# Two blocks of a transformer: retention's input projections moved into the steps of stick-breaking attention

## The chip, the cores and the metric

One core of a Trainium2 chip runs the whole program. The metric is the device time of one execution in microseconds; the median of the runs is compared. The five engines are called TensorE (PE in the profile; PEld is its weight load), VectorE (DVE), ScalarE (ACT), GpSimd (POOL) and SyncE (SP, which here only issues DMAs).

## The reference, cut to what matters

Two transformer blocks over 512 tokens of width 1024 in fp32. The part around the change is the mixing layer of the second block: one projection to 3584 columns, which are seven groups of 512, then two kinds of attention with eight heads of 64 each.

```python
xn = _rmsnorm(x, g_mix_norm)
proj = xn @ w_in                       # sb_q sb_k sb_v r_q r_k r_v r_g, 512 columns each
q_a, k_a = _rmsnorm(heads(sb_q)), _rmsnorm(heads(sb_k))
# stick-breaking, per head and block of 128 queries:
z = q_a @ k_a.T / 8;  mask = key < query
lneg = where(mask, log_sigmoid(-z), 0)
w = where(mask, exp(log_sigmoid(z) + reverse_cumsum(lneg) - lneg), 0);  y_a = w @ sb_v
q_b = _rope(_rmsnorm(heads(r_q)));  k_b = _rope(_rmsnorm(heads(r_k))) / 8
y_b = _group_norm(_retention(q_b, k_b, heads(r_v))) * silu(r_g)
x = x + concatenate([y_a, y_b]) @ w_out
```

After it come a top-4 mixture of 32 experts and a gated embedding. Before it comes the first block (two attentions and an MLP).

## The kernel before, in words

The program is one core's five instruction streams, written out by hand, with semaphores between them. Each engine works its stream in order. The 512 tokens are four tiles of 128 (NT). Matrix products of the projections are made in three parts: the operands are split into a top and a remainder (`half_top`, `ring_low`; `hT_top`, `hT_low`) and `three` (L1473) issues top times top, top times remainder and remainder times top.

**The projection.** The weights of one group of 512 columns are a chunk ("win2", c), 2 MB, loaded by SP into slots 0 and 1 of a ring in turn (`place`). A slot is loaded again when the chunk in it has been multiplied. Each chunk has two halves of four row blocks. ScalarE makes a half's top (`top`, L1033, four ACTIVATEs at L1043), VectorE its remainder in place (`low`, L2117, four instructions at L2126), and TensorE multiplies (`project`, L1479): four products of three parts for each of the four token tiles, 48 products a half, 96 a chunk. The tops lie in pairs of places listed in `TOP_AT`. Each of the four results has a PSUM bank, from which ScalarE copies it to SBUF with the row's norm factor (`copy_out`, L989, its ACTIVATE at L995).

The order of the chunks (`IN2`) is stick-breaking's q and k, retention's q and k, stick-breaking's v, retention's v and g. The loop over the seven chunks stands at L1785 (TensorE) and L1264 (ScalarE). After the fourth chunk TensorE turns stick-breaking's q and k into columns (`pairs_T`, "sbT"), which ScalarE copies to sbqT and, in halves of 64 partitions, to sbkz (L1282). After the seventh it turns retention's q and k ("rT"), copied to rqT and rkT. VectorE meanwhile normalises the heads (`heads`, L2150: square, sum, reciprocal of the root that ScalarE takes in `roots`, product), multiplies retention's by their gains (L2561), turns them (`rope`, L2160, six instructions of 128x256 a tile) and takes the mean off retention's v (L2577 to L2579).

**Stick-breaking attention** is `attention(2, ...)` on three engines. It runs over steps s = 0 to 40. In step s, TensorE makes the scores of step s (L1607; query tile t = s // 8, head s % 8, (t+1) x 128 keys), turns the weights of step s-3 (t+1 transposes, L1524) and multiplies those of step s-5 with v (L1625). VectorE adds the mask to the scores (L2208) and, in `stick` (L2173), scans (L2181) and multiplies (L2182) for step s-1. ScalarE takes two sigmoids of step s (L1082, L1083) and copies the turned weights of step s-4 (L1090). At each eighth step VectorE copies a tile's outputs (L2221), TensorE turns them ("oT"), ScalarE makes their top (L1106) and VectorE their remainder (L2141).

**What sets the order.** The list `order` gives each PSUM result a bank by hand or in rotation; `acquire` makes TensorE wait until the result before it in this bank has been taken. In this attention the scores have banks 0, 1, 2, 6 in turn, the transposes 3 and 4, the outputs 5 and the turned outputs 7. The buffers of the scan (sbl, sbw) are four each. While steps 1 to 8 run, VectorE also multiplies retention's k and turned q by their decay (`while_sticking`, L2586). ScalarE's Silu of the gate (L1288) stands ahead of the attention.

**Around it.** SP loads the embedding's tokens and weights (ptok, ple) when the last chunk has been multiplied, and the norm rows (gnrow) and the first output chunk when the last score has been made. GpSimd sets parts of sbkz to zero after the fourth chunk and of the retention's states after the sixth. After the attention TensorE turns the tokens, then does the retention's scores (`ret_scores`, L1806).

## Time and profile before

| what | value |
|---|---|
| runs | 2386.22, 2377.54, 2377.66 us |
| median | 2377.66 us |
| span of the profiled execution | 2375.5 us, from its first to its last instruction |
| its own time | not listed apart; the two lower runs are 2.0 and 2.2 us above this span |
| TensorE busy | 2239.7 us, 94% |
| VectorE busy | 1808.9 us, 76% |
| ScalarE busy | 1393.7 us, 59% |
| GpSimd busy | 209.7 us, 9% |
| mean granted TensorE clock | 0.967 |

The profile comes from one execution. A record of a matmul begins when it starts and ends by a model, so neighbouring records overlap and a pace is read from starts. The granted clock is a share of full speed, 1.00 being 2.4 GHz and 0.50 being 1.2 GHz. The seven chunks are projected from about 756 to 913 us, stick-breaking attention runs from 917 to 986 us, the retention after it to about 1030 us, and the experts take the time from about 1120 to 2330 us.

### The profile page before, as it was taken

Reading aid. Unit: us, or ns where it says so; the run is one execution under the profiler, and the core shown is the slowest. Engines: PE = TensorE matmul, PEld = TensorE weight load, DVE = VectorE, ACT = ScalarE, POOL = GpSimd, SP = SyncE. Lnnn points to the kernel's source line nnn. Section 1 sums busy time; section 2 is a strip of 40 time slices with the busy share of each in tenths; the row PEclk is TensorE's granted clock in tenths of the full one; section 3 lists DMA queues with packets and bytes.
Section 4 is the critical chain, followed back from the end, with each engine's and each line's share of the span. In section 5 each row is a group of like instructions: output and inputs, shape, how many; then the busy total and the mean of one; then the engine's idle time right before and its main releaser. Section 6 shows DMA issues by size and latency. Waiting matters only on the chain.

```text
span 2375.5 us, 30478 instructions
## 1 busy us (share of the span) xinstructions
PE 2239.7 (94%) x10453; PEld 1808.7 (76%) x10453; DVE 1808.9 (76%) x1917; ACT 1393.7 (59%) x1564; POOL 209.7 (9%) x175
## 2 busy tenths in 40 slices
PE   5998897999999998976999999999999999999998
PEld 3866676888788886755788888888888888888866
DVE  7887635555634585766899999999999999999964
ACT  4355525333413344433778778778778778778753
POOL 1000000000000000000241111011111111111100
PEclk8999798999999998987999999999999999999999
DMA  9530312333022310154999999999999999999960
GB/s 336 178 128 1 124 36 74 103 107 102 32 98 71 122 71 27 54 173 165 370 394 392 385 390 377 392 386 385 386 386 386 388 382 387 386 384 382 387 240 36
DMA packets 185074, 570.40 MB, mean 240 GB/s; under 512 B 10508, under 2 KB 34991, under 8 KB 184975
## 3 DMA queue, kind: packets, MB, share of 16 engines
q1 hardware_dynamic: 172239, 523.69, 57.6%
q0 software_dynamic: 12768, 45.81, 7.0%
q8 instruction: 43, 0.70, 0.1%
q14 instruction: 24, 0.20, 0.0%
HBM read 543.24 MB, written 26.23 MB: 240 GB/s over the span
## 4 chain that ended last, share of the span: by engine, by line
PE 51%; DVE 1%; issue 1%; ACT 0%; DMA 0%; ACTq 0%; DVEq 0%; POOLq 0%
PE bank L1936 11%; PE bank L1938 11%; PE bank L1942 11%; PE bank L1931 4%; PE bank L1929 4%; PE bank L1930 4%; PE bank L1524 3%; PE bank L1957 1%; PE bank L1543 0%; PE bank L1544 0%; PE bank L1545 0%; PE bank L2018 0%; PE bank L2012 0%; DMA rows<-hn_rows,idx_in 0%; PE bank L1980 0%
## 5 line engine op out<-in xcount | busy, mean ns | idle before, releaser
L2712 DVE TENSOR_TENSOR w_lo<-stage,w_hi 128x2048 fp32r<-128x2048 f32 x396 | 885.7, 2285 | 55.2 <-ACT w_hi L1342 55.2
L1342 ACT ACTIVATE w_hi<-stage 128x2048 fp32r<-128x2048 f32 x396 | 740.5, 1920 | 80.8 <-PE bank L1942 52.5
L1936 PE MATMUL bank<-w_hi,xeT_hi 128*128 128x512 f32 x792 | 261.7, 412 | 0.0
L1938 PE MATMUL bank<-w_hi,xeT_lo 128*128 128x512 f32 x792 | 245.8, 391 | 0.0
L1942 PE MATMUL bank<-w_lo,xeT_hi 128*128 128x512 f32 x792 | 212.2, 390 | 0.0
L1545 PE MATMUL bank<-half_top,hT_low 128*128 128x512 f32 (+1 forms) x480 | 187.9, 391 | 0.0
L1938 PEld LDWEIGHTS bank<-w_hi,xeT_lo 128*128 128x128 f32 x792 | 149.4, 189 | 32.5
L1936 PEld LDWEIGHTS bank<-w_hi,xeT_hi 128*128 128x128 f32 x792 | 147.6, 190 | 33.7 <-issue 0.3
L1942 PEld LDWEIGHTS bank<-w_lo,xeT_hi 128*128 128x128 f32 x792 | 149.1, 188 | 31.1
L1543 PE MATMUL bank<-half_top,hT_top 128*128 128x512 f32 (+1 forms) x416 | 162.7, 391 | 5.0 <-DVE ring_low L2128 2.2
L1544 PE MATMUL bank<-ring_low,hT_top 128*128 128x512 f32 (+1 forms) x416 | 161.8, 389 | 0.0
L1745 PE MATMUL bank<-hT_hi,up_hi 128*128 128x512 f32 x352 | 137.8, 392 | 7.0 <-issue 7.0
L1747 PE MATMUL bank<-hT_hi,up_lo 128*128 128x512 f32 x352 | 137.7, 391 | 0.0
L1746 PE MATMUL bank<-hT_lo,up_hi 128*128 128x512 f32 x352 | 137.6, 391 | 0.0
L2128 DVE TENSOR_TENSOR ring_low<-ring,half_top 128x2048 fp32r<-128x2048 f32 (+2 forms) x28 | 61.0, 2186 | 99.7 <-ACT half_top L1045 99.5
L1045 ACT ACTIVATE half_top<-ring 128x2048 fp32r<-128x2048 f32 (+2 forms) x28 | 51.0, 1829 | 139.2 <-PE bank L1545 134.7
L1936 PE MATMUL bank<-w_hi,eaT_hi 128*128 128x512 f32 x396 | 125.0, 397 | 0.9 <-DVE eaT_lo L2784 0.9
L1938 PE MATMUL bank<-w_hi,eaT_lo 128*128 128x512 f32 x396 | 122.0, 389 | 0.0
L1545 PEld LDWEIGHTS bank<-half_top,hT_low 128*128 128x128 f32 x480 | 91.9, 191 | 18.3
L1942 PE MATMUL bank<-w_lo,eaT_hi 128*128 128x512 f32 x396 | 105.8, 389 | 0.0
L1352 ACT ACTIVATE el<-bank,one 128x512 f32<-128x512 f32 x66 | 45.5, 689 | 98.3 <-PE bank L1931 98.3
L1931 PE MATMUL bank<-w_lo,xeT_hi 128*128 128x512 f32 x264 | 102.8, 389 | 0.0
(495 smaller groups left out, 4213.2 us busy)
## 6 DMA issues: line engine op xcount, KB each, us to landing
stage<-in_w_up_gate SPq DMA_DIRECT2D x264, 1024.0 KB, 7.4
stage<-in_w_down SPq DMA_DIRECT2D x132, 1024.0 KB, 7.3
ring<-in_w_ada SPq DMA_DIRECT2D x12, 2048.0 KB, 9.4
ring<-in_w_up SPq DMA_DIRECT2D x22, 1024.0 KB, 7.7
ring<-in_w_in SPq DMA_DIRECT2D x10, 2048.0 KB, 7.9
ring<-in_w_out SPq DMA_DIRECT2D x4, 2048.0 KB, 11.0
ring<-in_w_down SPq DMA_DIRECT2D x4, 2048.0 KB, 8.6
stage<-in_w_ple_gate SPq DMA_DIRECT2D x4, 1024.0 KB, 7.8
```

Of the source, the lines that this page charges most:

```text
L1342: fn(w_hi[top_of(h)][:, :], src[:, :], ACT.Copy).then_inc(s_hi, 1)
L1543: mm(b, hi, wh, start=first, stop=False)
L1544: mm(b, hi, wl, start=False, stop=False)
L1545: return mm(b, lo, wh, start=False, stop=last)
L1745: mm(b[:, :], wh, hTs[0][:, k, :], start=k == 0, stop=False)
L1746: mm(b[:, :], wh, hTs[1][:, k, :], start=False, stop=False)
L1747: ins = mm(b[:, :], wl, hTs[0][:, k, :], start=False, stop=k == KT - 1)
L1931: ins = mm(bank[b][:, :], hi[:, k0 + k, :], wl[:, k, cs], start=False, stop=k == kn - 1)
L1936: mm(bank[b][:, :], hi[:, k0 + k, :], wh[:, k, at_[b]:at_[b] + CW], start=first and k == 0, stop=False)
L1938: mm(bank[b][:, :], lo[:, k0 + k, :], wh[:, k, at_[b]:at_[b] + CW], start=False, stop=False)
L1942: ins = mm(bank[b][:, :], hi[:, k0 + k, :], wl[:, k, at_[b]:at_[b] + CW], start=False, stop=False)
L2712: tt(w_lo[h][:, :], stage[h][:, :], w_hi[top_of(h)][:, :].bitcast(FP), ALU.subtract).then_inc(s_lo, 1)
```

## The change

The three chunks of stick-breaking attention (q, k, v) are projected first, as before. The four chunks of retention (q, k, v, g) are then projected inside the attention's steps 0 to 31: `BESIDE` gives each step one chunk, half and token tile, twelve products, which TensorE issues at the end of its step. ScalarE's copies, tops and two roots, and VectorE's remainders, norms, gains, rotations and mean, are spread over the steps too. So that banks 2, 4, 6 and 7 are free for the four results of a chunk, scores have banks 0 and 1, transposes bank 3, and turned outputs bank 1. The scan's buffers are two instead of four. ScalarE copies the turned weights ahead of its two sigmoids. The turned outputs of the first three tiles are stored (`stick_out`) and split at steps 34 and 35. Retention's q and k are turned in steps 36 and 37, the decays follow in VectorE's steps 38 and 39, and Silu stands in ScalarE's step 33. SP's waits read as before, though the last chunk that they name now ends with step 31.

```diff
@@ -209,13 +209,13 @@
+    sbl = [at(R + (8 + 2 * i) * KB, [P, S], name=f"sbl{i}") for i in range(2)]
+    sbw = [at(R + (12 + 2 * i) * KB, [P, S], name=f"sbw{i}") for i in range(2)]
+    stick_out = [at(R + (84 + 2 * i) * KB, [P, 4, P], name=f"stick_out{i}") for i in range(3)]
...
-    sbl = [at((32 + 2 * i) * KB, [P, S], name=f"sbl{i}") for i in range(4)]
-    sbw = [at((88 + 2 * i) * KB, [P, S], name=f"sbw{i}") for i in range(4)]
@@ -356,7 +356,7 @@
-    IN2 = [0, 1, 3, 4, 2, 5, 6]
+    IN2 = [0, 1, 2, 3, 4, 5, 6]
@@ -429,19 +429,30 @@
+    BESIDE = [(c, h, t) for c in range(3, 7) for h in range(2) for t in range(NT)]
+    TURNED = {36: 0, 37: 1}
+    RQ_AT = (9, 10, 12, 13, 14, 15, 16, 18)
+    RK_AT = (19, 20, 22, 23, 24, 25, 26, 29)
...
-                product(("S", kind, s), (0, 1, 2, 6)[s % 4] if kind == 2 else s % 3)
+                product(("S", kind, s), s % 2 if kind == 2 else s % 3)
...
-                product(("T", kind, i), 3 + i % 2)
+                product(("T", kind, i), 3 if kind == 2 else 3 + i % 2)
...
-                product(("oT", kind, (s - OT_LAG[kind]) // H - 1), 7)
+                product(("oT", kind, (s - OT_LAG[kind]) // H - 1), 1 if kind == 2 else 7)
+            if kind == 2 and s < len(BESIDE):
+                c, h, t = BESIDE[s]
+                if h == 0:
+                    product(("win2", c, t), (2, 4, 6, 7)[t])
+            if kind == 2 and s in TURNED:
+                for t in range(NT):
+                    product(("rT", TURNED[s], t), ((2, 4, 6, 7) if TURNED[s] == 0 else (0, 4, 6, 7))[t])
@@ -494,16 +505,12 @@
-    for c in range(7):
+    for c in range(3):
...
-        if c == 3:
-            for qk in range(2):
-                for t in range(NT):
-                    product(("sbT", qk, t))
...
-            product(("rT", qk, t))
+            product(("sbT", qk, t))
@@ -1088,6 +1085,17 @@
+                    if kind == 2 and s < 4 * H:
+                        n = (s // H + 1) * P
+                        W1 = sbl[s % 2]
+                        act_e.wait_ge(s_msk, s + 1)
+                        b = bank[bank_of[("S", 2, s)][0]]
+                        if s >= 2:
+                            act_e.wait_ge(s_P, 4 * H + s - 1)
+                        if s >= 4:
+                            full(act_e, ("T", 2, s - 4))
+                        fn(PR[s % 4][:, 0:n], b[:, 0:n], ACT.Sigmoid)
+                        take(fn(W1[:, 0:n], b[:, 0:n], ACT.Sigmoid, scale=-1.0), ("S", 2, s))
@@ -1101,6 +1109,8 @@
+                elif kind == 2 and t < 3:
+                    take(fn(stick_out[t][:, :, :], blk3(b[:, :]), ACT.Copy), label)
@@ -1261,32 +1271,55 @@
-            for c in range(7):
-                if c < 6:
-                    top(("win2", c + 1), 0)
+            def mix_rows(c, t):
+                copy_out(win2_dst(c, t), ("win2", c, t), scale=stat[:, 48 + t:49 + t])
+            for c in range(3):
+                top(("win2", c + 1), 0)
...
-                    copy_out(win2_dst(c, t), ("win2", c, t), scale=stat[:, 48 + t:49 + t])
-                if c < 6:
-                    top(("win2", c + 1), 1)
-                if c < 3:
+                    mix_rows(c, t)
+                top(("win2", c + 1), 1)
+                if c < 2:
...
-                if c == 3:
-                    act_e.wait_ge(s_qs, 1)
+            act_e.wait_ge(s_qs, 1)
+            for t in range(NT):
+                copy_out(sbqT[:, :, t * P:(t + 1) * P], ("sbT", 0, t), lambda b: blk3(b[:, :]), qs[:, 0:1])
+            for t in range(NT):
+                label = ("sbT", 1, t)
+                b = full(act_e, label)
+                for par in range(2):
+                    hp = slice(par * HD, (par + 1) * HD)
+                    ins = fn(sbkz[hp, par::2, t * P:(t + 1) * P], blk3(b[hp, :]), ACT.Copy, scale=vec[hp, VSK:VSK + 1])
+                take(ins, label)
+            def while_sticking(s):
+                if 1 <= s <= len(BESIDE):
+                    c, h, t = BESIDE[s - 1]
+                    if h:
+                        if (c, t) == (6, 0):
+                            act_e.wait_ge(s_nrm, 9)
+                        mix_rows(c, t)
+                if s % 8 == 0 and 8 <= s < 32:
+                    top(("win2", 3 + s // 8), 1)
+                if s % 8 == 4 and s < 24:
+                    top(("win2", 4 + s // 8), 0)
+                if s in (11, 20):
+                    roots(7 + s // 20)
+                if s == 33:
...
-                        copy_out(sbqT[:, :, t * P:(t + 1) * P], ("sbT", 0, t), lambda b: blk3(b[:, :]), qs[:, 0:1])
+                        taken(act_e, ("win2", 6, t))
+                    fn(rg[:, :, :], rg[:, :, :], ACT.Silu).then_inc(s_sg, 1)
+                if s == 34:
+                    full(act_e, ("win2", 6, NT - 1))
+                    for t in range(3):
+                        fn(out_top[0][:, :, t * P:(t + 1) * P], stick_out[t][:, :, :], ACT.Copy).then_inc(s_ohi, 1)
+                if s - 1 in TURNED:
+                    qk = TURNED[s - 1]
...
-                        label = ("sbT", 1, t)
-                        b = full(act_e, label)
-                        for par in range(2):
-                            hp = slice(par * HD, (par + 1) * HD)
-                            ins = fn(sbkz[hp, par::2, t * P:(t + 1) * P], blk3(b[hp, :]), ACT.Copy, scale=vec[hp, VSK:VSK + 1])
-                        take(ins, label)
-                    roots(8)
-            for qk in range(2):
-                for t in range(NT):
-                    copy_out(rT[qk][:, :, t * P:(t + 1) * P], ("rT", qk, t), lambda b: blk3(b[:, :]))
-            fn(rg[:, :, :], rg[:, :, :], ACT.Silu).then_inc(s_sg, 1)
-            attention(2, PR2, PT2)
+                        copy_out(rT[qk][:, :, t * P:(t + 1) * P], ("rT", qk, t), lambda b: blk3(b[:, :]))
+            attention(2, PR2, PT2, while_sticking)
@@ -1782,21 +1815,39 @@
-            for c in range(7):
+            for c in range(3):
...
-                if c == 3:
-                    for qk, src in enumerate((sbq, sbk)):
-                        pe.wait_ge(s_nrm, 6 + qk)
-                        pairs_T("sbT", qk, src)
-            for qk, src in enumerate((rq, rk)):
-                pe.wait_ge(s_nrm, 8 + qk)
-                pairs_T("rT", qk, src)
+            for qk, src in enumerate((sbq, sbk)):
+                pe.wait_ge(s_nrm, 6 + qk)
+                pairs_T("sbT", qk, src)
...
+            def while_sticking(s):
+                if s < len(BESIDE):
+                    c, h, t = BESIDE[s]
+                    label = ("win2", c, t)
+                    if t == 0:
+                        pe.wait_ge(s_low, half_no[("win2", c), h] + 1)
+                    _, wl, wh, kn, n = half_cols(("win2", c), h)
+                    b = bank[bank_of[label][0]] if h else acquire(label)
+                    for k in range(kn):
+                        kk = h * kn + k
+                        ins = three(b[:, 0:n], of(hT_top[2])(kk, t), of(hT_low)(kk, t), wh[:, k * n:(k + 1) * n], wl[:, k * n:(k + 1) * n], kk == 0, kk == KT - 1)
+                    if h:
+                        publish(ins, label)
+                    elif t == NT - 1:
+                        ins.then_inc(s_read, 1)
+                if s in TURNED:
+                    qk = TURNED[s]
+                    pe.wait_ge(s_nrm, 8 + qk)
+                    pairs_T("rT", qk, (rq, rk)[qk])
...
-                      lambda h, j: sbv[:, j, h * HD:(h + 1) * HD], PR2, PT2, o2)
+                      lambda h, j: sbv[:, j, h * HD:(h + 1) * HD], PR2, PT2, o2, while_sticking)
@@ -1864,6 +1915,7 @@
+            pe.wait_ge(s_olo, NT + 3)
@@ -2136,6 +2188,9 @@
+                if kind == 2 and t < 3:
+                    tt(hT_low[:, 0:4, cols_t], stick_out[t][:, :, :], out_top[0][:, :, cols_t].bitcast(FP), ALU.subtract).then_inc(s_olo, 1)
+                    return
@@ -2174,10 +2229,10 @@
-                W1, W2, A = sbl[s % 4], sbw[s % 4], PR2[s % 4]
+                W1, W2, A = sbl[s % 2], sbw[s % 2], PR2[s % 4]
...
-                if s >= 4:
-                    dve.wait_ge(s_P, 4 * H + s - 3)
+                if s >= 2:
+                    dve.wait_ge(s_P, 4 * H + s - 1)
@@ -2224,7 +2279,7 @@
-                    if kind and s >= H + OT_LAG[kind] and (s - OT_LAG[kind]) % H == 0:
+                    if kind and s >= H + OT_LAG[kind] and (s - OT_LAG[kind]) % H == 0 and (kind == 1 or s == 4 * H + OT_LAG[kind]):
@@ -2552,45 +2607,78 @@
-                low(("win2", 2 + j), 0, 1)
-            for j, (a, c) in enumerate(((rq, 2), (rk, 3))):
-                for t in range(NT):
-                    taken(dve, ("win2", c, t))
-                link(heads(7 + j, a, tmpr, scale=None if j == 0 else HD ** -0.5))
+                if j == 0:
+                    low(("win2", 2), 0, 1)
+                else:
+                    low(("win2", 3), 0)
+            rvh = rv[:, :, :].rearrange("p t (h d) -> p (t h) d", d=HD)
+            vmean = hs[:, 4 * 32:5 * 32]
+            rk3 = rk[:, :, :].rearrange("p t (h d) -> p t h d", h=H)
+            def ret_heads(j, n):
+                a, c = ((rq, 3), (rk, 4))[j]
+                st = hs[:, (7 + j) * 32:(8 + j) * 32]
...
-                link(tt(flat, flat, bc(grow2[:, j, :], 1, [P, 32, HD]), ALU.mult))
-                low(("win2", 4 + j), 0)
-                for t in range(NT):
+                squares = tmpr[:, :].rearrange("p (n d) -> p n d", d=HD)
+                if n == 0:
+                    for t in range(NT):
+                        taken(dve, ("win2", c, t))
+                    link(tt(squares, flat, flat, ALU.mult))
+                elif n == 1:
+                    link(ve.reduce_sum(st, squares, axis=AX))
+                    ts(st, st, 1.0 / HD, EPS, ALU.mult, ALU.add).then_inc(s_ms, 1)
+                elif n == 2:
+                    dve.wait_ge(s_rt, 8 + j)
+                    link(ve.reciprocal(st, st))
+                    if j:
+                        link(ts(st, st, HD ** -0.5, None, ALU.mult))
+                    link(tt(flat, flat, bc(st, 2, [P, 32, HD]), ALU.mult))
+                elif n == 3:
+                    link(tt(flat, flat, bc(grow2[:, j, :], 1, [P, 32, HD]), ALU.mult))
+                elif n < 4 + NT:
+                    t = n - 4
...
-                ins.then_inc(s_nrm, 1)
-                dve.wait_ge(s_nrm, 8 + j)
-                low(("win2", 4 + j), 1)
-            low(("win2", 6), 0, 1)
-            for t in range(NT):
-                taken(dve, ("win2", 5, t))
-            rvh = rv[:, :, :].rearrange("p t (h d) -> p (t h) d", d=HD)
-            vmean = hs[:, 4 * 32:5 * 32]
-            link(ve.reduce_sum(vmean, rvh, axis=AX))
-            link(ts(vmean, vmean, 1.0 / HD, None, ALU.mult))
-            link(tt(rvh, rvh, bc(vmean, 2, [P, 32, HD]), ALU.subtract))
-            for t in range(NT):
-                full(dve, ("rT", 1, t))
-            rk3 = rk[:, :, :].rearrange("p t (h d) -> p t h d", h=H)
-            for t in range(NT):
-                taken(dve, ("rT", 0, t))
+                    else:
+                        ins.then_inc(s_nrm, 1)
+                        dve.wait_ge(s_nrm, 8 + j)
...
-                if 1 <= s <= NT:
-                    t = s - 1
-                    tt(rk3[:, t], rk3[:, t], bc(cb("kdec"), 2, [P, H, HD]), ALU.mult).then_inc(s_kd, 1)
-                elif NT < s <= 2 * NT:
-                    cols_t = slice((s - NT - 1) * P, (s - NT) * P)
-                    tt(rqdT[:, :, cols_t], rT[0][:, :, cols_t], blk3(cb("qdec")), ALU.mult).then_inc(s_rqd, 1)
+                if s % 8 == 1 and s < 26:
+                    low(("win2", 3 + s // 8), 1)
+                if s % 8 == 5 and s < 24:
+                    low(("win2", 4 + s // 8), 0)
+                if s in RQ_AT:
+                    ret_heads(0, RQ_AT.index(s))
+                if s in RK_AT:
+                    ret_heads(1, RK_AT.index(s))
+                if s == 27:
+                    for t in range(NT):
+                        taken(dve, ("win2", 5, t))
+                    link(ve.reduce_sum(vmean, rvh, axis=AX))
+                    link(ts(vmean, vmean, 1.0 / HD, None, ALU.mult))
+                if s == 28:
+                    link(tt(rvh, rvh, bc(vmean, 2, [P, 32, HD]), ALU.subtract))
+                if s == 35:
+                    full(dve, ("win2", 6, NT - 1))
+                    for t in range(3):
+                        out_low(2, t)
+                if s == 38:
+                    for t in range(NT):
+                        taken(dve, ("rT", 0, t))
+                    for t in range(NT):
+                        cols_t = slice(t * P, (t + 1) * P)
+                        tt(rqdT[:, :, cols_t], rT[0][:, :, cols_t], blk3(cb("qdec")), ALU.mult).then_inc(s_rqd, 1)
+                if s == 39:
+                    for t in range(NT):
+                        full(dve, ("rT", 1, t))
+                    for t in range(NT):
+                        tt(rk3[:, t], rk3[:, t], bc(cb("kdec"), 2, [P, H, HD]), ALU.mult).then_inc(s_kd, 1)
```

## Rows read from the trace of the kernel before

**Rows 1.** Busy time of each engine while one chunk is projected; last: clock, DMA share, GB/s

```profile
821.30:843.00 21.70, 21.70 (x98) 17.94 (x97) 17.88 (x21) 7.98 (x13) 0.00 (x0) 1.00 0.28 97
```

**Rows 2.** The same view in stick-breaking attention

```profile
916.60:931.80 15.20, 6.21 (x31) 4.93 (x29) 9.05 (x26) 9.43 (x23) 0.00 (x0) 0.65 0.17 69
...
959.00:975.60 16.60, 15.55 (x92) 10.23 (x91) 15.50 (x24) 11.41 (x25) 0.00 (x0) 1.00 0.01 1
...
975.60:988.80 13.20, 11.54 (x84) 10.36 (x82) 6.79 (x10) 6.11 (x12) 0.00 (x0) 0.90 0.57 200
```

**Rows 3.** Waits from 912 to 990 us: total us, times, longest

```profile
PE bank L1524 <- DVE probs L2182: 7.3, 5, 6.0
...
PE bank L1524 <- ACT probsT L1090: 6.0, 10, 2.1
```

**Rows 4.** Timeline, TensorE: start, us, engine, line, instruction, count

```profile
907.79 0.39 PE L1543 MATMUL bank<-half_top,hT_top 128*128 128x512 f32 x1
...
908.47 0.39 PE L1543 MATMUL bank<-half_top,hT_top 128*128 128x512 f32 x1
...
914.98 1.91 PE L1524 MATMUL bank<-cona,rk 128*128 128x128 f32 x16
...
973.10 1.08 PE L1607 MATMUL bank<-sbkz,sbqT 128*128 128x512 f32 x2
...
982.37 2.85 PE L1625 MATMUL bank<-sbv,probsT 128*128 128x64 f32 x24
```

**Rows 5.** Timeline, VectorE in the attention's steps

```profile
924.31 0.29 DVE L2208 TENSOR_TENSOR bank<-bank,conb 128x128 f32<-128x128 f32 x1
...
925.16 0.68 DVE L2590 TENSOR_TENSOR rk<-rk,conb 128x512 f32<-128x512 f32 x1
...
967.41 1.22 DVE L2181 TENSOR_TENSOR_SCAN sbw<-sbl,one 128x512 f32<-128x512 f32 x1
...
969.50 1.22 DVE L2181 TENSOR_TENSOR_SCAN sbw<-sbl,one 128x512 f32<-128x512 f32 x1
```

**Rows 6.** Timeline, VectorE beside the projection

```profile
829.42 2.29 DVE L2146 TENSOR_REDUCE hs<-tmpr 128x32 f32<-128x2048 f32 x1
...
837.26 2.74 DVE L2126 SCALAR_TENSOR_TENSOR ring_low<-ring,vec,half_top 128x512 fp32r<-128x512 f32 x4
...
839.92 0.42 DVE L2166 TENSOR_TENSOR tmpr<-rq,trig 128x256 f32<-128x256 f32 x1
...
842.67 0.43 DVE L2166 TENSOR_TENSOR tmpr<-rq,trig 128x256 f32<-128x256 f32 x1
```

**Rows 7.** Timeline, ScalarE: copies, a half's top, and the turned keys

```profile
821.28 0.69 ACT L995 ACTIVATE rq<-bank,stat 128x512 f32<-128x512 f32 x1 [2.03 <-PE bank L1545]
...
843.63 2.55 ACT L1043 ACTIVATE half_top<-ring,vec 128x512 fp32r<-128x512 f32 x4
...
848.36 5.61 ACT L1282 ACTIVATE sbkz<-bank,vec 64x512 f32<-64x512 f32 x8
```

**Rows 8.** Timeline, ScalarE: Silu and the table load behind it

```profile
919.34 1.91 ACT L1288 ACTIVATE rg<-rg 128x2048 f32<-128x2048 f32 x1
...
921.27 1.28 ACT L1082 ACT_TABLE_LOAD   x1
```

**Rows 9.** Busy times by stretch, after TensorE's idle time at 1054 to 1062

```profile
1064.00:1068.00 4.00, 4.00 (x10) 3.09 (x10) 3.93 (x9) 1.43 (x1) 0.00 (x0) 0.50 0.00 0
```

**Rows 10.** Timeline, TensorE after two idle times (in brackets)

```profile
1062.34 0.80 PE L1543 MATMUL bank<-half_top,out_top 128*128 128x512 f32 x1 [8.22 <-DVE ring_low L2128]
...
1152.46 0.60 PE L1957 MATMUL bank<-bias,hot 96*128 96x512 bf16 x2 [3.61 <-DVE hot L2861]
...
1155.09 1.05 PE L1938 MATMUL bank<-w_hi,xeT_lo 128*128 128x512 f32 x2
```

**Rows 11.** DMA issues by line: count, KB each, us to landing

```profile
ring<-in_w_in SPq DMA_DIRECT2D x10, 2048.0 KB, 7.9
```

**Rows 12.** Timeline, TensorE: the first retention scores

```profile
988.81 2.02 PE L1806 MATMUL bank<-rqT,rkT 64*128 64x128 f32 x16
```

25 lines of the change are left out of this document (7 added, 18 removed).

## The prediction

> **What bounds the kernel now.** I read the busy shares by stretch first. While the second block's seven 512-column chunks are projected, TensorE never rests: a chunk of 96 products takes 21.7 us at full clock [rows 1]. From 916.7 to 988.8 us, in stick-breaking attention, it does rest: 9 of the first 15.2 us, 1 of the 16.6 us with the widest tiles, less than 2 of the last 13.2 [rows 2]. The waits name the cause: the transposes (L1524) wait for VectorE's product of probabilities (L2182) and for ScalarE's copy out of the transposes' bank (L1090) [rows 3]. So the two stages have opposite limits, and about 72.1 us of attention hold some 15 us of idle TensorE at most. I take 821.3 us (end of the third chunk's products) to 988.8 us (first retention score), 167.5 us, as the stretch that the change rebuilds; before it nothing moves on TensorE, and after it the same work follows.
>
> **TensorE's own work.** Products start every 0.227 us, three in 0.68, and each is 0.39 long, so a group's record ends up to 0.2 after its pace. With that off, 16 transposes in 1.91 are 0.11 each, the score of four blocks of 128 columns in 1.08 is 0.22 a block, and 24 PV products in 2.85 are 0.115 each, two to a block, 0.23 [rows 4]. A step of query tile t (0 to 3) has t+1 blocks of each, 0.56(t+1), and twelve products, 2.72 us plus about 0.03. With the transposes three steps behind and PV five behind, the eight steps of each tile take 25.0, 29.5, 34.5 and 39.0 us: **128.0 us** for 32 steps.
>
> **VectorE's work per step.** Mask, scan and product recur every 0.86 us for one block (924.31 to 925.16) and 2.09 for four [rows 5]; between them 1.27 and 1.66 by the width. To that the change adds, per step: a half's remainder (seven halves, one at each of steps 1, 5, 9, 13, 17, 21, 25) 2.66; a pass over 128x2048 2.3, at 9, 10, 12, 13 for the queries, 19, 20, 22, 23 for the keys, 27 and 28 for the values; a tile's rotation 2.75, at 14, 15, 16, 18 and 24, 25, 26, 29 [rows 6]. Sums per eight steps, with 0.8 for each copy of the outputs: 11.6, 31.4, 34.7, 35.6 us, against TensorE's 25.0, 29.5, 34.5, 39.0. These passes were free before (they lay under the chunks' products); now VectorE is as full as TensorE from step 8 on. ScalarE has 9 to 20 us per eight steps, but in lumps: a half's top takes 2.55 us [rows 7], and each of the two roots inside the steps needs a table load of 1.28 before it and one before the next sigmoid [rows 8].
>
> **How tightly they are tied.** All transposes now share bank 3 (before 3 and 4). Transpose s-3 in step s needs transpose s-4 copied out. ScalarE makes that copy first in its own step s, after its step s-1, whose sigmoids need VectorE's mask of s-1, which stands behind everything VectorE does in step s-2, passes included. The other new ties are looser: a sigmoid waits for the product two steps back (two scan buffers), scores 17 and 25 for the copy of the turned outputs in bank 1, ScalarE in step 29 for the keys' last rotation, with the row copies and the next sigmoids queued behind it, which need VectorE's next mask anyway, and TensorE's output projection for three remainders from step 35. A lump on VectorE is thus lent for hardly more than one step, and a wait of TensorE on it holds the twelve products queued behind. If a step costs the longest of the three engines' sums, the excess over TensorE is 0.8 in steps 1 and 5; 7.2 in 8 to 15 (2.8 at step 9, where VectorE has 6.3 to do against 3.5; 2.4 at 13; 1.1 at 12); 1.7 in 16 to 23; 3.5 in 24 to 31 (2.9 at 25, 7.5 against 4.7). Sum 13.2, so **141.2 us**. If a lump can be spread over two steps, the sums of pairs give 135.2; nothing spread away gives 141.2, everything hidden 128.0. I take 141.2, as the single bank speaks for it, and keep both others.
> The Trainium skill has a rule against this part of the change: Perfetto Trace Analysis, Optimizing Tensor Performance, says that independent matmul groups should rotate through PSUM banks, so that copying out of one overlaps the next group. By the rule the loss is real; without it the sum would be the 128.0. The 6.0 us that the transposes wait for L1090, with two banks, point its way.
>
> **The start.** Attention now needs the turned queries and keys directly after the third chunk. ScalarE copied the last rows out at 821.28 for 0.58 us, then it has the next half's top, four copies sbqT and eight sbkz; in the old trace that row of work runs from 843.63 to 853.97, 10.34 us [rows 7]. So the first score is at 832.2, and TensorE idles 7 to 8 us after its 32 transposes. This was hidden under the next chunk. The clock pays too: after an idle of 8.22 us the granted clock was 0.50, its lower level of 1.2 GHz, for the first 5.7 us of products [rows 9, 10], at 0.427 instead of 0.227 us each: 2.7 us lost. Nothing else in the start is late: the third chunk's remainder and the key norm end earlier in the old trace, the zeroing on POOL waits for chunk 1 instead of 3.
>
> **The tail.** Step 31 ends at 832.2 + 2.7 + 141.2 = 976.1. From there one chain: last rows copied out 0.9, copy of transpose 29 0.6, table load and Silu 3.2 [rows 8], copy of transpose 30 0.6, three copies of stored outputs 1.7, copy of transpose 31 0.6, PV 0.9, sixteen transposes of the queries 1.8, their last copy 0.7, then VectorE's two passes in four parts of 0.68 each, 5.5 [rows 5], which were hidden before: 16.6, say **17 us**. The keys' transposes are beside it. SP now issues the tokens, the embedding weights, the norm rows and the first output chunk after chunk 6, at about 976 instead of 913: 4 MB, two chunks' worth; a chunk lands in 7.9 us [rows 11], so 16 at most, inside the 17. The state's zeroing on POOL is long done. TensorE waits in three pieces here; half of the 3 us that the clock was low in the old tail [rows 2] again, 1.5. First retention score at 994.6.
> One more fall of the clock is open: after an idle of 3.61 us a pair of products still took 1.05 us at 1155 [rows 10]; I take 5 us at half speed, 2.5 lost. The walk leaves one wait near that size at steps 25 to 30; counted half, 1.2. That makes 995.8, against 988.8 [rows 12]: **+7.0 us**. The sum is made against the profiled execution (span 2375.5, about 2.2 us less than the two lower runs' times); on the median of 2377.66 it is 2384.7. Later stages get the same shift: they start from the retention's end, and none of their inputs is earlier or later against it.
>
> **Rivals.**
> First, TensorE-bound as meant: the lumps are absorbed, 832.2 + 2.7 + 128.0 + 15 (the tail with fewer waits) = 977.9, **-10.9 us**, 2366.8. For it: VectorE's sum is below TensorE's over the whole, 113 against 128. Against it: the single bank. The skill's page TensorE: Matmul & The Clock Gate, Loop structure matters more than you think, says that copying results out on VectorE does no harm as long as the products stay back to back; by that rule this case comes out.
> Second, **slower by over 0.5%**: the clock falls in the uneven stretches. Its place is steps 9 to 15, 17 to 22 and 25 to 30; its price 2.5 us each time, 7.5 on 994.6 is 1002.1, +13.3, 2391. It decides from a single idle of about 3.6 us on; the old attention's waits for L1090 were up to 2.1 us long [rows 3], and its widest tiles kept 1.00 [rows 2], which speaks against it.
> Third, nothing arrives: the stretch's gain or loss is swallowed by the experts' weight stream, 0 us, 2377.7. Against it, the stream starts only after the retention's products.
>
> **Numbers.** Step-locked forecast 0.52; TensorE-bound 0.22; clock falls 0.21; swallowed 0.05. The 0.5% that a measurement can tell is 11.9 us. The first rival stands 1 us short of it, so a bit less than half of it, 0.10, is faster; slower is the second and 0.03 of the forecast's upper end, 0.24; the rest 0.66. The range runs from the first rival's number to a little past the second, 2367 to 2394.
>
> **What would show it.** Right: first score at 832, first PV chain slow; steps 9, 13 and 25 the longest of their tiles, their transposes waiting for L1090; 141 us for 32 steps; the first retention score 17 to 19 us after the last product. Wrong: steps of even length with no wait before transposes (first rival), or a granted clock under 1 between steps 9 and 31 (second). If VectorE shows idle time in steps 9 to 30, the tie is looser than I take it.

## The result and the profile after

The changed kernel is **slower**: 2396.7 us, median of 5 runs (2394.11 to 2399.54), against 2377.66 us; the ratio is 1.0067, 95% interval 1.0051 to 1.0082. The two medians alone are 19.0 us apart, 0.80%, and the five runs before lie in two groups, 2375.3 to 2377.7 and 2385.4 to 2386.2. The prediction had 2384.7 us and gave no change the larger chance, 0.66, against 0.24 for slower. The profiled execution is the slowest of the five, 2399.54 us with a span of 2397.7, 22.2 us above the span before.

Not all of that is the change's. The tile view of the first copies of stick-breaking's queries, which come before anything in the program that differs, already shows 5.2 us between the two executions (before at the top, after below; the last numbers are first and last start):

```profile
L995 ACT ACTIVATE sbq<-bank,stat x4: 690/690/692, 769.6 to 777.8; 128x512 f32<-128x512 f32 x4
```

```profile
L1002 ACT ACTIVATE sbq<-bank,stat x4: 690/690/690, 774.8 to 783.0; 128x512 f32<-128x512 f32 x4
```

This step stands between executions of the same code too (two of the kernels below, changed only behind this point, stood at 774.9 and 769.7), so I take it off in every comparison: the change costs 17.0 us in this profile, and 0.67% of 2377.66, 15.9 us, in the runs. The retention's scores, last row below, start at 1006.45 instead of 988.81: +17.6, **+12.4** with the step taken off, where I had +7.0. The other 4.6 come behind it: 1.3 up to the last retention score, 0.3 on balance up to the experts and 3.0 in them, where the old kernel with the copy first, below, lost 2.2 with no change there. I leave those open.

Busy times of the changed kernel for steps 0 to 7, 8 to 15, 16 to 23, 24 to 31 and the tail behind them (columns as in [rows 1]):

```profile
837.80:865.40 27.60, 26.98 (x124) 22.42 (x125) 11.91 (x30) 9.50 (x29) 0.00 (x0) 0.94 0.00 1
865.40:898.30 32.90, 30.05 (x149) 24.27 (x148) 28.01 (x46) 16.72 (x39) 0.00 (x0) 1.00 0.19 65
898.30:938.70 40.40, 36.16 (x177) 28.65 (x176) 35.42 (x58) 20.57 (x42) 0.00 (x0) 0.96 0.15 52
938.70:983.70 45.00, 40.69 (x200) 31.25 (x199) 36.55 (x59) 17.74 (x33) 1.84 (x6) 0.96 0.00 1
983.70:1006.40 22.70, 17.24 (x101) 16.60 (x99) 7.68 (x14) 13.46 (x21) 0.00 (x0) 0.70 0.50 185
```

The 32 steps last 145.9 us (837.8 to 983.7), forecast 141.2. VectorE is busy 112 of them (forecast 113), so its work was right; TensorE idles 12. Against [rows 2] the sides have changed: now the clock falls in the steps and, above all, in the tail. TensorE's waits from 837 to 1007 us:

```profile
PE bank L1557 <- ACT probsT L1087: 15.3, 10, 3.7
PE bank L1640 <- ACT sbkz L1292: 7.8, 1, 7.8
PE bank L1857 <- DVE rk L2681: 2.2, 1, 2.2
```

The first line is the tie of [rows 3]'s L1090, 6.0 us before, with one bank instead of two. Two of its places explain it. First VectorE's timeline about step 17 (the last instruction of a rotation, then the mask), then ScalarE's, then TensorE's:

```profile
900.39 0.43 DVE L2226 TENSOR_TENSOR rq<-tmpr 128x256 f32<-128x256 f32 x1
900.86 0.30 DVE L2263 TENSOR_TENSOR bank<-bank,conb 128x128 f32<-128x128 f32 x1
```

```profile
901.19 0.49 ACT L1097 ACTIVATE probs<-bank 128x384 f32<-128x384 f32 x1 [2.51 <-DVE bank L2263]
901.58 0.48 ACT L1098 ACTIVATE sbl<-bank 128x384 f32<-128x384 f32 x1
901.95 0.60 ACT L1113 ACTIVATE stick_out<-bank 128x512 f32<-128x512 f32 x1
902.43 0.70 ACT L1002 ACTIVATE rk<-bank,stat 128x512 f32<-128x512 f32 x1
903.00 2.57 ACT L1050 ACTIVATE half_top<-ring,vec 128x512 fp32r<-128x512 f32 x4
905.45 0.39 ACT L1087 ACTIVATE probsT<-bank 128x256 f32<-128x256 f32 x1
```

```profile
905.98 0.63 PE L1557 MATMUL bank<-cona,probs 128*128 128x128 f32 x2 [2.45 <-ACT probsT L1087]
```

ScalarE waited 2.51 us for VectorE's mask, which stood behind a pass; then came its own lump, two copies and a top, 3.5 us (901.95 to 905.45), and only then the copy that frees bank 3. One engine's lump stands behind the other's, and the single bank hands the sum to TensorE. At step 30 the order is the same with one lump, the rotation of the keys on which ScalarE's row copy waits:

```profile
971.74 0.69 ACT L1002 ACTIVATE rg<-bank,stat 128x512 f32<-128x512 f32 x1 [3.39 <-DVE rk L2226]
972.33 0.59 ACT L1087 ACTIVATE probsT<-bank 128x512 f32<-128x512 f32 x1
```

```profile
973.06 0.63 PE L1557 MATMUL bank<-cona,probs 128*128 128x128 f32 x4 [3.73 <-ACT probsT L1087]
```

The granted clock after these waits and in the tail:

```profile
906.00:908.00 2.00, 2.00 (x8) 1.90 (x9) 1.97 (x5) 0.98 (x3) 0.00 (x0) 0.50 0.00 0
...
974.00:976.00 2.00, 2.00 (x9) 1.71 (x9) 0.00 (x0) 1.06 (x2) 0.00 (x0) 0.57 0.03 8
...
990.00:1000.00 10.00, 8.84 (x42) 8.87 (x43) 2.59 (x4) 4.51 (x9) 0.00 (x0) 0.50 0.68 253
```

And TensorE's timeline in the tail, with the waits in brackets:

```profile
987.45 0.64 PE L1557 MATMUL bank<-cona,probs 128*128 128x128 f32 x4 [1.84 <-ACT probsT L1087]
...
991.16 1.09 PE L1557 MATMUL bank<-cona,probs 128*128 128x128 f32 x4 [1.46 <-ACT probsT L1087]
...
997.05 3.62 PE L1557 MATMUL bank<-cona,rq 128*128 128x128 f32 x16
...
1006.45 0.79 PE L1857 MATMUL bank<-rqT,rkT 64*128 64x128 f32 x5 [2.21 <-DVE rk L2681]
```

The sixteen transposes take 3.62 us where [rows 4] have 1.91: this is the lower level, 1.2 GHz. The tail is 22.7 us, from 983.7 to 1006.45.

### The profile page after: what moved, and what is told of

It reads as the page before. It is cut to its first block, busy times and chain, and to the rows that moved or that the text cites. A ratio compares the mean times of both kernels' runs of the same rounds, so it can differ in the third digit from the quotient of the medians.

```text
span 2397.7 us, 30537 instructions
## 1 busy us (share of the span) xinstructions
PE 2251.7 (94%) x10453; PEld 1823.1 (76%) x10453; DVE 1809.1 (75%) x1917; ACT 1399.5 (58%) x1571; POOL 204.0 (9%) x175
## 4 chain that ended last, share of the span: by engine, by line
PE 85%; DVE 8%; ACT 3%; issue 2%; DMA 1%; SPq 1%; DVEq 0%; ACTq 0%; POOLq 0%
PE bank L1988 11%; PE bank L1990 11%; PE bank L1994 11%; PE bank L1576 6%; PE bank L1577 6%; PE bank L1578 6%; PE bank L1557 4%; PE bank L1983 4%; PE bank L1982 4%; PE bank L1981 4%; PE bank L1778 3%; PE bank L1779 3%; PE bank L1780 3%; PE bank L1658 2%; PE bank L1640 2%
## 5 line engine op out<-in xcount | busy, mean ns | idle before, releaser
L1576 PE MATMUL bank<-half_top,hT_top 128*128 128x512 f32 (+1 forms) x416 | 167.9, 404 | 4.0 <-DVE ring_low L2180 2.2
## 6 DMA issues: line engine op xcount, KB each, us to landing
ring<-in_w_out SPq DMA_DIRECT2D x4, 2048.0 KB, 11.8
```

The costliest lines, as they stand in the source:

```text
L1576: mm(b, hi, wh, start=first, stop=False)
```

## The experiments

All are compared with the changed kernel by stage: the 32 steps, the tail, the first retention score (FRS) and the last (LRS), each with the step before 770 us taken off.

**VectorE's passes left out.** In `ret_heads` and `while_sticking`:

```diff
-                    link(tt(squares, flat, flat, ALU.mult))
+                    pass
...
-                    ins = rope(a4[:, :, 0:hw], a4[:, :, hw:], trig2, t, tmpr, [P, H, hw])
...
-                    link(tt(rvh, rvh, bc(vmean, 2, [P, 32, HD]), ALU.subtract))
```

> Left out: VectorE's passes over retention's queries, keys and values inside the steps (squares, sums, norm, gain, rotation, mean); its remainders, masks, scans and products stay, as do all waits. So only the stretch from the first score to the first retention score is compared, not the total. In the changed kernel the 32 steps take 146.0 us (first score 837.8, end of step 31 983.7), and the transposes wait 15.3 us in ten pieces for the copy of the transposes before. Theory (steps are locked to the longest engine, and VectorE's passes make the lumps): without them VectorE's sum is under TensorE's in every step but 1 and 5, so the steps take 128.0 + 0.8 and a little for ScalarE's 2.6 us tops, 129 to 132 us; the waits of transposes for the copy fall under 4 us, and the granted clock stays at 1.00 between steps 2 and 31. Rival A (ScalarE's lumps, its tops ahead of the next copy, make the waits): 140 us or more remain, with the waits at steps 12, 16, 20. Rival B (the twelve products between the matmuls of attention cost more than their own pace): no waits, but still 140 us.

The score of step 31 starts at 967.7 instead of 978.8 and its step lasts 4.95, so the steps take 134.8 us: **11.1 less**, the expected direction and 3 short of the size. Most of it comes at two places, each a wait with the low clock behind it: 3.4 us in step 17 and 5.5 in step 30. From 842 on the clock stays at 1.00 throughout the steps. The waits in the steps, 12.0 us in eight places in the changed kernel, are now:

```profile
PE bank L1557 <- ACT probsT L1087: 4.7, 6, 1.7
```

The 4.7 that are left stand behind ScalarE's own lumps, five times a top and once a root with its table loads (1.66); at 902.5 its top of 2.57 ends half a microsecond before the transposes start. So Rival A has a share, under 5 us, and the passes the larger one; Rival B falls. The FRS is 11.8 us earlier, the LRS only 7.0: behind it the clock was low from 995 to 1008.

**Two banks for the transposes.**

```diff
-                product(("T", kind, i), 3 if kind == 2 else 3 + i % 2)
+                product(("T", kind, i), 3 + 4 * (i % 2) if kind == 2 else 3 + i % 2)
...
-                        ins = three(b[:, 0:n], ..., kk == 0, kk == KT - 1)
+                        ins = three(b[:, 0:n], ..., kk == (4 if t == 3 else 0), kk == KT - 1)
```

> The transposes of the weights have banks 3 and 7 in turn instead of 3 alone. Changed for it: the first half of the fourth token tile's twelve products a chunk is added into bank 2 beside other sums and not kept; the count, the shape and the place of all products stay. Compared is the stretch of the 32 steps, 146.0 us in the changed kernel. Theory (the one bank ties TensorE to ScalarE's copy of the step before): the waits of transposes for the copy, 15.3 us in ten pieces, fall under 4, and the sums of pairs of steps decide, 135.2 instead of 141.2: steps 135 to 139 us. Rival (the copy is late because the masks and scans are, so with two banks TensorE waits for VectorE's product or for the PV copy instead): steps within 2 us of 146, the waits under another name.

TensorE's waits in the steps:

```profile
PE bank L1642 <- ACT sbkz L1294: 7.8, 1, 7.8
PE bank L1578 <- ACT rk L1004: 4.7, 1, 4.7
PE bank L1578 <- ACT rv L1004: 1.9, 1, 1.9
PE bank L1578 <- ACT rq L1004: 1.5, 1, 1.5
```

The waits of transposes for the copy are gone from the steps, as expected. The last score comes 5.0 us earlier, so the steps take 140.9 us, where I expected 135 to 139; FRS 7.2 earlier, LRS 8.7. My edit made a wait of its own: bank 2 now carries two tiles' results, and TensorE stood 8.1 us for their row copies (the three lower rows), with the clock at 0.60 behind the longest of them. So I read the 5.0 as a lower bound of what the second bank is worth. Here the rule of the Trainium skill, Perfetto Trace Analysis, Optimizing Tensor Performance, that independent groups should rotate through banks so that copying out of one overlaps the next, agrees with the trace: the waits went with the second bank, and the row copies' 8.1 us came with a shared one.

**The old kernel with one bank** for the transposes and two for the scores, to see what the banks cost where nothing else is moved; only the two lines of the order change:

```diff
-                product(("S", kind, s), (0, 1, 2, 6)[s % 4] if kind == 2 else s % 3)
+                product(("S", kind, s), s % 2 if kind == 2 else s % 3)
...
-                product(("T", kind, i), 3 + i % 2)
+                product(("T", kind, i), 3 if kind == 2 else 3 + i % 2)
```

> The kernel before, with no product moved, but stick-breaking's scores in banks 0 and 1 and its transposes in bank 3 alone, as the changed kernel has them. Its attention then lasts 72.1 us from first score to first retention score with two banks of transposes and four of scores. Theory (the one bank costs where a lump stands ahead of the copy; here ScalarE and VectorE have hardly any lump, only the decays in steps 1 to 8, but TensorE has nothing else to do either, and is itself the one that waits): 0 to 4 us more, in the first two tiles. Rival A: the one bank costs by itself, 8 us or more, as in the changed kernel. Rival B: nothing at all, under 0.5 us.

2459.03 us against 2383.05. Attention takes 152.9 us (917.1 to 1070.0) instead of 72.1. Of my cases only Rival A's "8 us or more" covers that, and its reason, a bank that costs by itself, falls with the next run. One step of it, first VectorE, then ScalarE, then TensorE:

```profile
965.10 0.30 DVE L2208 TENSOR_TENSOR bank<-bank,conb 128x128 f32<-128x128 f32 x1 [2.90 <-PE bank L1607]
```

```profile
965.43 0.49 ACT L1082 ACTIVATE probs<-bank 128x384 f32<-128x384 f32 x1 [3.31 <-DVE bank L2208]
965.82 0.48 ACT L1083 ACTIVATE sbl<-bank 128x384 f32<-128x384 f32 x1
966.19 0.39 ACT L1090 ACTIVATE probsT<-bank 128x256 f32<-128x256 f32 x1
```

```profile
963.47 1.59 PE L1607 MATMUL bank<-sbkz,sbqT 128*128 128x384 f32 x2
966.73 0.66 PE L1524 MATMUL bank<-cona,probs 128*128 128x128 f32 x2 [1.66 <-ACT probsT L1090]
```

Read it as a ring: score, mask, both sigmoids, copy, transpose, and only then the next score. I had overlooked that the old ScalarE step makes the copy last. From 937 to 1057 TensorE's clock was 0.50 to 0.59, which makes the ring longer still.

**The same with the copy first**, the changed kernel's order on ScalarE:

```diff
+                    i = s - (4 if kind == 2 else 2)
+                    if 0 <= i < 4 * H:
...
+                        take(fn(PT[i % 2][:, 0:i // H + 1, :], ..., ACT.Copy), ("T", kind, i))
                     if kind == 2 and s < 4 * H:
...
-                    i = s - (4 if kind == 2 else 2)
-                    if 0 <= i < 4 * H:
```

> The kernel before with one bank for the transposes and two for the scores, which alone made it 76 us slower, and now also the changed kernel's order on ScalarE: in each step the copy of the turned weights ahead of the two sigmoids. Theory (the cost of the one bank is set by what stands ahead of that copy; with the sigmoids ahead of it, transposes, copy, sigmoid, mask and next score form one ring around each step, 153 us for attention): with the copy first the ring is open, and attention takes 72 to 78 us from first score to first retention score, 0 to 6 us more than before. Rival (one bank costs by itself, whatever the order): 20 us or more above the kernel before.

Attention 73.1 us (923.1 to 996.2), 1.0 above before, and waits of transposes for the copy of 4.2 us in 10. Two things differ from the kernel before here, the banks and the order; the next run has the order alone.

> The kernel before with its own banks and the copy of the turned weights ahead of the sigmoids; nothing else. It had 6.0 us of transposes waiting for that copy. Theory: with two banks the order hardly matters, since the copy of one bank has a whole step; the waits shrink by 1 to 4 us, the total by 0 to 3. Rival: the sigmoids, now later by one copy (0.2 to 0.6 us), delay the scan, which is on the path in the narrow tiles: 1 to 5 us slower.

With the old banks and the copy first, attention takes 69.5 us (914.6 to 984.1), 2.6 less, and the waits for the copy are gone. **So, at the same order on ScalarE, the fewer banks cost 3.6 us with the copy first (73.1 against 69.5) and 80.8 with the copy last (152.9 against 72.1).** In the changed kernel the cost hangs on what stands ahead of the copy, and has no price of its own beyond the 5.0 us above. The scores' banks and the scan's buffers, two instead of four as well, were not tried apart, though no wait of TensorE in the changed kernel's steps names them. One run; the step before 770 us is 2.1 the other way here, so I read the stage, not the total of 2374.49.

**The start.** Queries turned behind the second chunk, the next half's top behind the keys' copies, half of these on VectorE:

```diff
+        if c:
+            for t in range(NT):
+                product(("sbT", c - 1, t))
...
+            take(fn(sbkz[0:HD, 0::2, ...], blk3(b[0:HD, :]), ACT.Copy, ...), label)
+            top(("win2", 3), 1)
...
+                ts(sbkz[HD:P, 1::2, ...], blk3(b[HD:P, :]), vec[HD:P, VSK:VSK + 1], None, ALU.mult).then_inc(s_kc, 1)
```

> Stick-breaking's queries are turned behind the second chunk instead of the third, the half top of the fourth chunk follows the copies of the keys instead of standing ahead of them, and VectorE makes half of those copies. In the changed kernel TensorE idles 7.8 us before the first score at 837.8 and the clock is at or under 0.71 for six microseconds after it. Theory: ahead of the first score stand only the last rows and four copies of 0.8 us, so the idle is 1 to 3 us, the first score 5 to 7 us earlier (the 16 transposes of 1.9 us only change places), the clock stays up (1.7 us more), and the whole gain, 7 to 9 us, is still there at the first retention score, since the steps are locked to one another and not to the start. Rival: the steps wait for the later half top or for VectorE, which is now later by 3 us of copies, and step 31 ends at most 3 us earlier.

The wait ahead of the first score is 1.8 us instead of 7.8; first score 6.0 us earlier (825.5, with 1.1 the other way before 770), FRS 4.3 earlier, LRS 5.9. The expected sign, but half the size: the clock's 1.7 us, which the steps have up to step 21, are gone at step 22, and the tail is no shorter.

**Keeping TensorE busy.** 58 transposes of a constant in the first wait, 12 at the end of steps 33 to 35:

```diff
+            for _ in range(58):
+                tr(bank[bank_of[("sbT", 0, 0)][0]][:, 0:P], cona[:, 0:P])
...
+                if 33 <= s <= 35:
+                    for _ in range(12):
+                        tr(bank[0][:, 0:P], cona[:, 0:P])
```

> The changed kernel with transposes of a constant that nobody reads, only to keep TensorE busy: 58 (6.7 us at 0.115 each) in its 7.8 us of idle time ahead of the first score, and 12 (1.4 us) at the end of each of steps 33, 34 and 35. Theory (part of the loss is the clock: at or under 0.71 for six microseconds after the first idle, at 0.50 from 988 to 1001 in the tail): the granted clock is 1.00 at the first score, 1.5 to 2 us are won there, and 3 to 4 in the tail: first retention score 4 to 6 us earlier. Rival (the clock's stretches lie under waits for ScalarE and VectorE): under 1.5 us, or later, where the added transposes delay the needed ones.

The clock was 1.00 at the first score, and the scores of steps 1 to 21 came 1.5 to 1.7 us earlier. In step 21, after the same wait of 1.78 us as in the changed kernel, the clock fell here (0.50 from 927 to 929) and not there, and the gain was gone. The FRS came 1.4 us earlier in all, the LRS 4.9 later. The rival is nearer: in the tail the waits are for copies and for the decays, and behind the wait of 2.88 us for these the clock stayed low:

```profile
1006.00:1021.00 15.00, 15.00 (x67) 13.29 (x68) 7.63 (x15) 2.09 (x3) 0.00 (x0) 0.50 0.00 1
```

**Silu and the stored outputs later**, in ScalarE's steps 40 and 39, the remainders behind the keys' decay:

```diff
-                if s == 33:
+                if s == 4 * H + OT_LAG[2]:
                     for t in range(NT):
                         taken(act_e, ("win2", 6, t))
                     fn(rg[:, :, :], rg[:, :, :], ACT.Silu).then_inc(s_sg, 1)
```

> Silu of the gate (1.91 us, with the table load of 1.28 ahead of it) and the three copies of stored outputs (1.66 us) leave ScalarE's steps 33 and 34 for its steps 40 and 39, and VectorE's three remainders follow the keys' decay. In the changed kernel the end of step 31 at 983.7 is followed by the first retention score at 1006.45, 22.7 us. Theory (the tail is one chain through ScalarE, and its 4.85 us of Silu and copies lie on it): tail 22.7 - 4.9 = 17.9 us, and 1 to 2 less where the clock, low from 988 to 1001, stays up; 16.5 to 18, total 5 to 6 us less than the changed kernel. Rival (the tail is set by the low clock and by VectorE's two decays behind the transposes): 21.5 us or more, total within 1.5 us; or what is gained is lost again because Silu is late for the gate: first retention score early, retention's end not.

FRS 1.5 us earlier, LRS 5.6 later, the end 3.8 later (the execution was 5.1 us earlier before 770). My 4.9 us fell: with Silu away, ScalarE waits for PV (the products of the weights with v) and for transposes, at half clock from 985 to 990, and the decays follow these. After the wait of 2.82 us for the decays:

```profile
1000.00:1016.00 16.00, 15.68 (x66) 13.90 (x67) 9.01 (x17) 4.97 (x6) 0.00 (x0) 0.50 0.00 0
```

**The same work in other steps.** Steps 4 and 27 carry no products, so that the gate's last ones fall into the tail; the passes are spread; Silu and the stored copies stand later; the retention's scores don't wait for the decays:

```diff
+    PAUSES = (4, 27)
+    AT = [s for s in range(32 + len(PAUSES)) if s not in PAUSES]
+    TURNED = {35: 0, 36: 1}
+    RQ_AT = (9, 11, 12, 13, 15, 16, 17, 18)
+    RK_AT = (20, 21, 23, 24, 25, 26, 28, 29)
...
-            pe.wait_ge(s_kd, NT)
-            pe.wait_ge(s_rqd, NT)
             ret_scores(0)
-            ret_pairs(0)
             ret_scores(1)
+            pe.wait_ge(s_kd, NT)
+            pe.wait_ge(s_rqd, NT)
+            ret_pairs(0)
```

> The changed kernel with the same work in other steps: steps 4 and 27 carry no twelve products, so that the gate's last ones fall into steps 32 and 33; VectorE's passes stand at 9, 11, 12, 13, 15 to 18 and 20, 21, 23 to 26, 28, 29, the mean of v in 32; the queries and keys are turned a step earlier, Silu and the stored outputs' copies stand in ScalarE's step 38, and the retention's scores no longer wait for the decays, only the products of keys and values do. In the changed kernel: 32 steps with all products and the tail from 837.8 to 1006.45, 168.7 us. Theory (steps locked by VectorE's lumps, then a tail in which TensorE idles and the clock is low): the lumps spread save the 3.7 us wait at step 29 and some 2 us about steps 14 and 18; 5.4 us of products go under the tail and the decays' 5.0 us leave it: 12 to 18 us less, first retention score at 988 to 995, the end of the retention 8 to 14 us earlier. Rival A: the tail's time is the low clock, which falls whenever TensorE waits 2.5 us, and it only moves: under 6 us. Rival B: VectorE, with 113 us of work in the steps, is now behind at the end: waits for the decays' replace those for the copies, 5 to 8 us.

FRS 20.0 us earlier (more than the 12 to 18 expected), LRS 14.2, the end 17.2: with the old start, and with the step taken off, the kernel before to 1 us. The waits for the copy are 3.9 us in 5. Rival A falls for the steps, but is right behind them (see the next).

> The version before this one together with the earlier turned queries and the shared copies of the keys (which alone made the first score 6.1 us earlier and the end of the retention 6 us earlier, once the difference that stood before the change's first instruction is taken off). Theory: the gains add, since the one is ahead of the first score and the other behind it: first retention score 18 to 24 us earlier than in the changed kernel, total 14 to 20 us less than its 2397, 2377 to 2383: the kernel before, give or take 5 us. Rival: the start's gain is lost in the steps (VectorE's three microseconds of copies delay step 1), total as the version without it.

FRS 977.3, 29.2 earlier than in the changed kernel, more than the 18 to 24 expected; end 23.8 earlier, where the two parts alone had 17.2 and 7.4: at the end the gains add. Two rows remain of the tail's story:

```profile
PE bank L1860 <- DVE hT_low L2202: 4.8, 1, 4.8
```

```profile
984.00:997.00 13.00, 13.00 (x60) 11.30 (x60) 7.34 (x15) 2.66 (x4) 0.00 (x0) 0.59 0.00 0
```

The retention's second scores shared bank 1 with the last turned outputs, and the clock was low behind that.

**The bank of the last outputs, Silu straight from PSUM, and the stored outputs' copies in step 35.**

```diff
-                product(("oT", kind, ...), 1 if kind == 2 else 7)
+                product(("oT", kind, ...), 1 if kind == 2 and s < 4 * H + OT_LAG[kind] else 7)
...
+                            take(fn(rg[:, t, :], b[:, :], ACT.Silu, scale=stat[:, 48 + t:49 + t]), label)
```

> The combination (other steps for the passes and products, earlier start, scores not waiting for the decays) with three edits for the one wait left in its tail, 4.8 us of TensorE for VectorE's last remainder, because the retention's second scores have the bank of the last turned outputs, and after it 14 us at half clock: the last turned outputs get bank 7; Silu is taken from the PSUM bank with the row's factor in place of the copy and the pass over 128x2048; the stored outputs are copied in step 35 and their remainders follow in 36, where VectorE idled 8.8 us. Theory: the wait falls under 2 us, the clock stays up, the retention takes 22 to 25 us instead of 31.9, and the total falls 8 to 12 us under the combination's 2375.8, that is 2364 to 2368; against the kernel before a ratio of 0.992 to 0.997. Rival A: the clock falls anyway (after the wait for the decays of 1 to 2 us), and only 2 to 4 us are won, ratio 0.997 to 1.001. Rival B: the earlier copies and Silu delay the last transposes' copies, and first retention score comes 2 us later than 977.3.

2370.73 us, median of 6, against 2381.46 of 11 runs of the kernel before beside it: ratio **0.9957, interval 0.9940 to 0.9974**. It beats both kernels. Its profile began as the one before does (769.6), so its span of 2365.1 against 2375.5 says the same, 10.4 us. From first to first retention score it takes 146.8 us, the changed kernel 168.7. TensorE's waits to 1000 us, then busy times in the steps and in the retention:

```profile
PE bank L1560 <- ACT probsT L1091: 3.8, 5, 1.7
PE bank L1643 <- DVE sbkz L2624: 1.8, 1, 1.8
PE bank L1560 <- ACT rkT L1004: 1.0, 1, 1.0
```

```profile
826.60:939.00 112.40, 107.55 (x538) 86.04 (x539) 91.54 (x163) 58.55 (x130) 1.83 (x6) 1.00 0.14 51
939.00:973.40 34.40, 33.08 (x208) 27.46 (x207) 24.18 (x37) 18.72 (x34) 0.00 (x0) 1.00 0.20 74
...
980.00:990.00 10.00, 10.00 (x41) 6.99 (x41) 8.50 (x17) 3.28 (x5) 0.32 (x1) 0.69 0.00 0
```

No wait over 1.8 us is left up to there, and the clock is 1.00 until the retention begins. The ratio lies where it was expected. The 8 to 12 us below the combination don't: with that one's 5.2 before 770 taken off, the FRS is 1.3 later (Rival B's mechanism, inside its 2 us), the LRS 4.5 earlier, the end 3.6. Which of the three edits gave that was not taken apart.

## What was right and wrong in the prediction, step by step

**Where TensorE was the bound, and that VectorE would be level with it: right.** The steps' excess over TensorE's 128.0 is 17.9 us in the profile. The forecast had 13.2, by step-wise maxima. Sums per tile: 27.6, 32.9, 40.4, 45.0 measured, less 1.6 of clock in the first; forecast 25.8, 36.7, 36.2, 42.5.

**The step that failed is "If a step costs the longest of the three engines' sums".** In 8 to 15 it overstates by 3.8, which I read as VectorE's lump being partly lent. From 16 on it understates by 6.7: a maximum can't see one engine's lump stand behind the other's, as at 905, nor the clock's fall behind such a wait, some 3.4 of the 6.7. That the 32 steps were only 3.1 us off in the end is in part luck, since the two errors cancel. The places were wrong too: from step 8 on the longest steps are 12, 17 and 30 (5.0, 8.3 and 10.5 us), not 9, 13 and 25. VectorE did idle, some 18 of the 118 us of steps 8 to 31, but not as my sign had it, from a looser tie: it waited 16.5 us for scores, which stood behind TensorE's own work and waits. With the passes gone 11.1 us go, with two banks 5.0: the tie was the right mechanism, its size is that of a chain.

**"ScalarE in step 29 for the keys' last rotation ... which need VectorE's next mask anyway": wrong.** What stands behind that wait is the copy out of bank 3. It gave the longest wait, 3.73 us, and a fall of the clock.

**The start: right** to half a microsecond. First score 832.6 with the 5.2 taken off, forecast 832.2; 7.8 us idle, forecast 7 to 8. The clock behind it was at 0.50 to 840 and back at 1.00 by 842, and cost 1.6 instead of 2.7 (the score of step 1 came that much earlier with TensorE kept busy), and in both runs that saved it, it was lost again at step 22.

**The tail: mis-sized.** Forecast 17 and 1.5 for the clock, measured 22.7, 4.2 more. Its links were the right ones, and some had their size (Silu with its table load 3.2, the decays two times 2.5). Others had not: the last rows, forecast 0.9, were out 3.1 us after step 31, behind the copy of the turned outputs, which was not in the sum; PV and the sixteen transposes, forecast 0.9 and 1.8, took 2.5 and 3.4, for TensorE waited three times and the clock was at 0.50 for some 13 us, from 988 to 1001. Yet neither Silu's removal nor a busy TensorE shortened the tail by more than 1.5 us, and two banks by 2.2; other work in it, with scores that don't wait for the decays, took the most off.

**The second rival came on top of the first forecast.** I let the clock fall from a single idle of 3.6 us on; in the run it fell after 2.45 us at 906. My sum corrected: +7.0, less 1.1 for the start's clock, plus 0.4 for the start, plus 3.1 in the steps without that clock (144.3 against 141.2; by my estimate from the granted clock, two falls of four microseconds at about 0.57 take 3.4 of the steps' time), plus 4.2 in the tail, less the 1.2 set aside for one more fall, is 12.4; measured 12.4. These terms were sized after the result, so their sum is an account and not a test. Beside it the Trainium skill, TensorE: Matmul & The Clock Gate, A second HAM failure mode: psum-queue depth-cycling, tells of a kernel in which short idles between groups of matmuls made the clock swing; the rows of 906 and 974 above, 0.50 and 0.57 behind waits ahead of a group of transposes, agree with it.

**Chances.** Slower by over 0.5% came, to which I had given 0.24. The first rival, TensorE-bound at 128.0, fell, and the single bank was the reason together with what stands ahead of its copy. The range ended at 2394; the median is 2.7 above it, by the ratio's 2393.6 just inside.

## What to carry to other kernels

Before two stages with opposite limits are laid into each other, list for each shared bank what stands ahead of the copy that frees it, on the copying engine and, behind its waits, on the engine that feeds it, and add these lumps up; a maximum by step can't show them. Put the copy that frees a bank first in its engine's step, and spread lumps so that no two engines' fall together. Leave some of the independent products for the tail. The version that spreads the lumps and leaves products for the tail, with the earlier start, turned +0.67% into -0.43%.

## What the hardware showed that I had not expected

The clock's fall doesn't go with the length of one wait: it fell to 0.50 after 2.45 us at 906, stayed at 1.00 after 1.78 at 926 and fell after the same 1.78 in the run with TensorE kept busy and in the one with the earlier start. How long it stays low differs more: some 4 us after the wait of 2.21 us at 1006, 15 us and more after 2.88 and 2.82, with TensorE busy throughout. The retention gave that back: LRS minus FRS was 22.1 us before, 23.3 in the changed kernel after its 2.21, 28.2 with the passes left out after 2.77, and 30.5 and 29.7 in the runs with 2.82 and 2.88.
